# Products inside the attention steps, an out projection by halves of features, index scores inside chunks, rotations on GpSimd

## The reference, cut to what matters

```python
# layer 2 of the first model: chunked attention, 16 heads of 64
kv = rmsnorm(h, kv_norm_g) @ w_kv                  # [256, 2048]
q = (rmsnorm(h, b_norm_g) @ w_q) * 64 ** -0.5      # [256, 1024]
o = softmax(q @ k.T + bias) @ v;  h = h + o @ w_o
h = h + conv_ffn(rmsnorm(h, f_norm_g))
# second model, even layer: 8 "forgetting" heads and 8 sliding-window heads with sinks
fq, fk, fv, fgl, sq, sk, sv = split(h @ w_in)      # w_in [1024, 2312]
x = x + g_m * (concat(fox(fq, fk, fv, log_sigmoid(fgl)), swa(rope(sq), rope(sk), sv, sinks)) @ w_out)
# second model, odd layer: an index picks 64 keys for each query
q, k, v, iq, ik, iw = split(h @ w_in)              # w_in [1024, 2120]; q, k, iq, ik get rope
score = sum_over_8_index_heads(iw * relu(iq @ ik.T)); keys = top_k(score, 64)
x = x + g_m * (attention_over(keys) @ w_out)
x = x + g_f * mixture_of_experts(x)
# the gates g_*, shifts and scales of the second model: silu(c) @ ada_w + ada_b, 12288 columns
```

## Time and profile before

| | us |
|---|---|
| runs | 1716.73, 1739.09, 1742.68 |
| median | 1739.09 |
| the profiled execution | 1743.0 |
| its span | 1741.0 |
| mean granted TensorE clock in it | 0.909 of full |

### The profile page before, as it was taken

The page is one execution under the profiler, slowest core; times in us unless marked ns, Lnnn a source line. Parts: engine busy times, 40 slices in busy tenths (PEclk is TensorE's granted clock), DMA queues, the critical chain, the costliest instruction groups (busy, mean ns, idle before and its releaser), DMA issues.

```text
span 1741.0 us, 20071 instructions
## 1 busy us (share of the span) xinstructions
PE 1597.5 (92%) x7386; PEld 1316.0 (76%) x7387; DVE 1242.2 (71%) x1681; ACT 899.8 (52%) x1123; POOL 4.3 (0%) x16
## 2 busy tenths in 40 slices
PE   5899999988999999789899998969879999999995
PEld 4778877776878878678788887858767887788874
DVE  4757888655457887664678875684478888888887
ACT  4545553434346653444443334432357777777774
POOL 0000000000000000000000000000000000000000
PEclk9999999996699999895899999865789999999998
DMA  7544447663044448460267675310248888897882
GB/s 309 218 168 146 182 181 292 239 241 122 24 175 164 166 171 315 151 229 34 97 250 279 256 263 192 145 49 1 73 147 325 319 307 318 299 342 302 308 316 116
DMA packets 54264, 358.17 MB, mean 206 GB/s; under 512 B 7088, under 2 KB 8112, under 8 KB 13360
## 3 DMA queue, kind: packets, MB, share of 16 engines
q1 hardware_dynamic: 51392, 353.47, 54.6%
q0 software_dynamic: 144, 2.10, 0.3%
q10 hardware_dynamic: 2656, 1.64, 0.3%
HBM read 356.13 MB, written 1.05 MB: 205 GB/s over the span
## 4 chain that ended last, share of the span: by engine, by line
PE 74%; DVE 15%; ACT 5%; issue 5%; DMA 1%; PEldq 0%; DVEq 0%; PEld 0%; ACTq 0%; SPq 0%
PE ps L413 19%; PE ps L415 19%; PE ps L414 19%; DVE wlo L1293 5%; PE ps L572 4%; PE ps L592 3%; PE ps L581 2%; PE ps L775 2%; ACT whi L918 2%; PE ps L524 1%; DVE tok L1421 1%; DMA head_scratch<-w_s_dram 1%; DVE tok L1832 1%; PE ps L548 1%; ACT ps L930 1%
## 5 line engine op out<-in xcount | busy, mean ns | idle before, releaser
L1293 DVE TENSOR_TENSOR wlo<-raw,whi 128x2048 fp32r<-128x2048 f32 (+1 forms) x303 | 651.1, 2171 | 186.4 <-ACT whi L918 174.5
L918 ACT ACTIVATE whi<-raw 128x2048 fp32r<-128x2048 f32 (+1 forms) x303 | 546.8, 1822 | 294.2 <-PE ps L415 293.9
L413 PE MATMUL ps<-whi,xhi 128*128 128x512 f32 (+3 forms) x1360 | 537.5, 395 | 22.9 <-DVE xlo L1366 8.0
L415 PE MATMUL ps<-whi,xlo 128*128 128x512 f32 (+3 forms) x1360 | 526.4, 387 | 0.0
L414 PE MATMUL ps<-wlo,xhi 128*128 128x512 f32 (+3 forms) x1360 | 526.0, 387 | 0.0
L413 PEld LDWEIGHTS ps<-whi,xhi 128*128 128x128 f32 x1360 | 260.2, 191 | 80.0 <-DVE wlo L1293 12.0
L415 PEld LDWEIGHTS ps<-whi,xlo 128*128 128x128 f32 x1360 | 259.6, 191 | 52.4
L414 PEld LDWEIGHTS ps<-wlo,xhi 128*128 128x128 f32 x1360 | 260.7, 192 | 48.2
L413 PE MATMUL ps<-whi,ahi 128*128 128x512 f32 x440 | 178.3, 405 | 12.8 <-DVE wlo L1293 12.8
L414 PE MATMUL ps<-wlo,ahi 128*128 128x512 f32 x440 | 174.9, 398 | 0.0
L415 PE MATMUL ps<-whi,alo 128*128 128x512 f32 x440 | 174.8, 397 | 0.0
(11 more groups left out here) (230 smaller groups left out, 1265.9 us busy)
## 6 DMA issues: line engine op xcount, KB each, us to landing
raw<-stream_dram SPq DMA_DIRECT2D x318, 1024.0 KB, 5.2
raw<-stream_dram SPq DMA_DIRECT2D x30, 512.0 KB, 4.1
attn_scratch<-toep_dram POOLq DMA_DIRECT2D x1, 2048.0 KB, 7.9
raw<-stream_dram SPq DMA_DIRECT2D x2, 528.0 KB, 5.7
h<-x_dram SPq DMA_DIRECT2D x1, 1024.0 KB, 5.5
y<-tok SPq DMA_DIRECT2D x2, 512.0 KB, 2.7
head_scratch<-w_s_dram ACTq DMA_DIRECT2D x1, 512.0 KB, 18.5
gates<-fg_dram ACTq DMA_DIRECT2D x1, 512.0 KB, 21.7
```

What stands on the lines that cost most here:

```text
L413: pe.matmul(o, xh, wh, start=start, stop=False)
L415: return pe.matmul(o, xl, wh, start=False, stop=stop)
L918: act.activation(whi[:, q % SPL, 0:w], raw[:, s % RAW, 0:w], ACT.Copy).then_inc(sem("hi_done"), 1)
L1293: dve.tensor_tensor(wlo[:, q % SPL, 0:w], raw[:, s % RAW, 0:w], whi[:, q % SPL, 0:w].bitcast(F32), ALU.subtract).then_inc(sem("lo_done"), 1)
```

## The change

1. **Products inside the steps (C and E).** PE's `product` is cut into `begin` and `half` (one slot for one token tile, 12 matmuls). The projections are reordered so that what the first heads need comes first: q, then k and v by halves in C; window heads before forgetting heads in E. The chunks that only later heads need run inside the steps: 10 halves in steps 0 to 8 of C, 8 halves in steps 0 to 6 of E. Their results are copied out by ACT and transposed by PE inside the steps too. Since the pairs of banks 0 to 3 are now taken by products, scores and value products have one bank each (4 and 5), and `back` uses bank 6, which `turn` uses for every second head. ACT and DVE split the slots inside the steps, at the place `split(base + slots_before(halves, i) + SPL)`.
2. **Out projection by halves of features.** Its weights are stored so that the first two slots hold the 512 features of the first two groups of heads for both output chunks. Two of its eight halves run in steps 16 and 18, and `residual_out` adds the results.
3. **Index scores inside chunks (O).** The order is index keys (the chunk of 72 columns), index queries, k and v, q, q. The 16 index products come in four groups of four inside and behind the slots of the chunks of k and v and of the first q.
4. **Rotations on GpSimd.** The rotations of q and k in O (12 instructions of 128x128 and 24 of 128x256) and of one token tile in E (6 of 128x320) are done by POOL, and POOL also makes `wlo` of the two slots of the last chunk in O.
5. **The "a" slots** move: none is left in the out projections, fewer in kv and `e_in`, more in the two first down projections (8 each where there were 6) and in the down projection of E (10 of its 12 slots where there were 6).

In the diff, a line that is only "..." marks what is left out.

```diff
-O_ORDER = (3, 4, 0, 1, 2)
+O_ORDER = (4, 3, 2, 0, 1)
+KV_ORDER = (0, 2, 1, 3)
...
-        proj("gmlp_in", 2 * D, G_ORDER, layer=0, first=4)
-        proj("gmlp_out", D, layer=0)
+        proj("gmlp_in", 2 * D, G_ORDER, layer=0, with_ada=(3, 5, 7))
+        proj("gmlp_out", D, layer=0, with_ada=(1, 3))
         proj("up0", 2 * FF)
-        proj("down0", D, kt=FK, layer=0)
-        proj("kv", 2 * D, layer=0)
-        proj("q", D, layer=0)
-        proj("attn_out", D, layer=0)
+        proj("down0", D, kt=FK, layer=0, with_ada=(0, 1, 3, 4, 6, 7, 9, 10))
+        proj("q", D, layer=0, with_ada=(1, 3))
+        proj("kv", 2 * D, KV_ORDER, layer=0, with_ada=(1,))
+        proj("attn_out", D)
         proj("up1", 2 * FF)
-        proj("down1", D, kt=FK, layer=0)
+        proj("down1", D, kt=FK, layer=0, with_ada=(0, 1, 3, 4, 6, 7, 9, 10))
         assert not left[0]
-        proj("e_in", E_IN, E_ORDER, layer=1)
-        proj("e_out", D, layer=1)
-        proj("e_up", 2 * FF, layer=1)
-        proj("e_down", D, kt=FK, layer=1)
+        proj("e_in", E_IN, E_ORDER, layer=1, with_ada=(1, 3, 5))
+        proj("e_out", D)
+        proj("e_up", 2 * FF, layer=1, with_ada=range(1, 22, 2))
+        proj("e_down", D, kt=FK, layer=1, with_ada=(0, 1, 2, 3, 4, 6, 7, 8, 9, 10))
...
+        HALVES_C = {0: 2, 1: 1, 2: 1, 3: 1, 4: 1, 5: 1, 6: 1, 7: 1, 8: 1, 16: 1, 18: 1}
+        HALVES_E = {0: 2, 1: 1, 2: 1, 3: 1, 4: 1, 5: 1, 6: 1, 16: 1, 18: 1}
+        HALVES_O = {16: 1, 18: 1}
+        o_slots = [QAT["o_in"] + sum(len(slots_of(KT, w)) for _, w in chunks_of(O_IN, O_ORDER)[:n]) for n in range(6)]
+        POOL_LO = range(o_slots[4], o_slots[5])
+        def slots_before(halves, i):
+            return sum(k for step, k in halves.items() if step < i) // 2
...
+            def lo_of(q):
+                s = PL.s_of[q]
+                g.wait_ge(sem("lo_done"), s)
+                g.wait_ge(sem("hi_done"), q + 1)
+                g.tensor_tensor(wlo[:, q % SPL, :], raw[:, s % RAW, :], whi[:, q % SPL, :].bitcast(F32), ALU.subtract)\
+                    .then_inc(sem("lo_done"), 1)
+            g.wait_ge(sem("acc_free"), PL.cat["o_in"] + 3)
+            rotate(1024, 4)
+            g.sem_inc(sem("rot_k"), 1)
+            for q in POOL_LO:
+                lo_of(q)
+            for n in range(2):
+                g.wait_ge(sem("acc_free"), PL.cat["o_in"] + 4 + n)
+                rotate(n * W, 8)
+                g.sem_inc(sem("rot_q"), 1)
...
                 def scores(u):
-                    if u >= 2:
-                        pe.wait_ge(sem("att_m"), b + u - 1)
+                    if u:
+                        pe.wait_ge(sem("att_m"), b + u)
                     a = units[u]
                     for t in range(NT):
-                        m = pe.matmul(ps[:, 2 * sc + u % 2, parts(t)], a["q"][:, t * P:(t + 1) * P], a["k"][:, 0:(t + 1) * P],
-                                      start=True, stop=True)
+                        m = pe.matmul(ps[:, 4, parts(t)], a["q"][:, t * P:(t + 1) * P], a["k"][:, 0:(t + 1) * P], start=True, stop=True)
...
                 def values(u):
                     pe.wait_ge(sem("att_c"), b + u + 1)
-                    g = u // 4
-                    if u % 4 == 0 and g >= 2:
-                        pe.wait_ge(sem("att_on"), bg + g - 1)
+                    if u and u % 4 == 0:
+                        pe.wait_ge(sem("att_on"), bg + u // 4)
                     for t in range(NT):
...
+                out = []
                 for i in range(n + 3):
                     if i < n:
+                        if i == 8 and turned:
+                            pe.wait_ge(sem("tr_free"), T("tr"))
                         scores(i)
+                    work(i)
+                    if i == 16:
+                        pe.wait_ge(sem("att_o"), bg + 2)
+                        out = [begin(W, first=first), begin(W, first=first)]
+                        half(out[0], 0)
+                    if i == 18:
+                        half(out[0], 1)
                     if 0 <= i - 2 < n:
                         turn(i - 2)
                     if 0 <= i - 3 < n:
                         values(i - 3)
+                    if i in (7, 11, 15):
+                        back(i // 4 - 1)
+                    ends(i)
                 T.up("att", n)
+                half(out[1], 0)
+                back(3)
+                half(out[1], 1)
+                pe.wait_ge(sem("att_o"), bg + 4)
+                for t in range(NT):
+                    half(out[0], t)
+                for t in range(NT):
+                    half(out[1], t, early=t == 0)
...
+            def other_heads(i):
+                if i == 0:
+                    half(chunk_now[0], 0)
+                    half(chunk_now[0], 1)
+                if i in (1, 5):
+                    chunk_now[0] = begin(W)
+                if 1 <= i <= 8:
+                    half(chunk_now[0], (i - 1) % 2)
+            def other_keys(i):
+                if i in (2, 5):
+                    pe.wait_ge(sem("acc_free"), T("acc", 1))
+                if i == 10:
+                    pe.wait_ge(sem("acc_free"), T("acc"))
+                if i in (5, 6):
+                    two(TB, i - 3, i - 3)
+            attention(CHUNKED, OUT_C, pT_c, other_heads, other_keys, (5, 6))
...
+                    before(i)
+                    if i in (8, 12, 16):
                         hi(i // 4 - 2)
-                hi(2)
-                split(used[0] + SPL)
+                    if i < n:
+                        exps(i)
+                    split(base + slots_before(halves, i) + SPL)
+                    after(i)
...
                 for i in range(n + 3):
                     if i < n:
                         mask(i)
+                    if i in (8, 12, 16):
+                        lo(i // 4 - 2)
                     if 0 <= i - 2 < n:
                         copy(i - 2)
-                    if i >= 7 and i % 4 == 3:
-                        weigh(i // 4 - 1)
-                    if i >= 9 and i % 4 == 1:
-                        lo(i // 4 - 2)
-                weigh(3)
-                split(used[0] + SPL)
+                    if i in (6, 10, 14, 18):
+                        weigh((i - 6) // 4)
+                    split(base + slots_before(halves, i) + SPL)
...
-            rotate(W, 8)
-            dve.sem_inc(sem("rope_done"), 1)
             thr = lambda t: mx8[:, t, 7:8]
             both(lambda t, nk: dve.tensor_tensor(score[:, t, 0:nk], score[:, t, 0:nk], causal[:, S - nk:S], ALU.add))
             for n in range(TOPK // 8):
@@ -1719,10 +1918,6 @@
                 both(lambda t, nk: dve.max(mx8[:, t, :], src[:, t, 0:nk]))
                 if n < TOPK // 8 - 1:
                     both(lambda t, nk: dve.match_replace(left[:, t, 0:nk], mx8[:, t, :], src[:, t, 0:nk], GONE))
-                if n == 3:
-                    rotate(2 * W, 4)
-                    dve.sem_inc(sem("rope_done"), 1)
-            skip(1)
```

514 lines of the change are left out of this document (311 added, 203 removed).

## The result

| | before | changed |
|---|---|---|
| runs, us | 1716.73, 1739.09, 1742.68, 1742.17 | 1774.32, 1768.42, 1773.08, 1768.20 |
| median, us | 1740.63 | 1770.75 |
| profiled execution, its span, us | 1743.0, 1741.0 | 1774.32, 1772.6 |
| mean granted clock | 0.909 | 0.917 |

The changed kernel is slower: the ratio is 1.022, 95% interval 1.012 to 1.033, and nothing of the interval reaches 1 (whether it is slower by more than 2% the interval leaves open). The forecast was 1733, at most 1758. The kernel before falls in two groups of times, 1713 to 1717 us (12 of its 55 runs in all comparisons here, middle 1715) and 1738 to 1744 (the other 43); its trace and all its medians are from the upper one, and the ratio mixes the two. All four times of the changed kernel lie above all 55: 30 us above the median of the kernel before, and 56 above 1715.

The account below looks back on a forecast made before the run. PE was taken as the bound, through many small float32 matmuls at half clock. C +9, E -2, O +1.4 and "a" slots -2 sum to +6.4: 1736.6, or 1733 against the median; range 1718 to 1748, chance 0.53.

Parts of the forecast that it names:

- PE bound by small matmuls at half clock: Steps of C and O, also E: PE's rows busy nearly all the time at 0.50, a C step 3.58 us.
- halves that hold the clock: Steps 0 to 8 of C: product halves keep full clock, 18.6 us net where 27 before, +8.5.
- The waits where the cover ends: Step 9 in C and 7 in E: late mask behind a split no longer hidden by products, about 2.9 each.
- POOL's price: POOL's work taken at about twice DVE's time: 4.6 us for `wlo`, 0.8 a rotation.
- The wait for a third split in O: O: scores of head 2 wait for mask 1 behind a third split, coming about 1156.5, leaving +8.
- What the halves of the out projections cost: Steps 16 and 18: halves fill no idle time; the first meets half clock, -1.0 each in C and E.
- C, before the steps: C ahead of its attention steps: a shorter wait in the projections, +1.2, and less turning of blocks, +4.0.
- Other down projections have room: 0: Down projections other than E's: more "a" slots there cost nothing, 0.
- -2 for E's: Down projection of E: four more "a" slots at 3.1 make DVE busy 58.7 of 60 us, costing 2.
- O, +1.4: Stage O: earlier first mask leaves +8, less q rounds -2.2, two waits -3.9 and tail -0.5.
- POOL is late: Rival for O, chance 0.12: at four times DVE's prices POOL delays the first mask by 17 us, 1750.
- the clock stays up without products: Rival, chance 0.17: later steps of C and E stay at full clock after the products end, 1716.

Follow-up runs that it names:

- e2_csplit: Changed kernel with ACT making the next weight slot's high part ahead of each of two turned-block copies in C's q chunks; 1760.42 us.
- e5_turn: Changed kernel with PE's sum over an "a" slot pair made behind the first half of a weight slot, not the second; 1762.62 us.
- e1_plan: Changed kernel with four "a" slots moved from the down projection of E to its up projection; 1772.18 us.
- e3_dvelo: Changed kernel with both POOL `wlo` splits of O's last chunk given to DVE, inside its search; 1767.12 us.
- b1_plan: Kernel before with only the changed kernel's "a" slot places from E on; 1722.37 us.
- b2_plan: Kernel before with one "a" slot (behind slot 7) moved from E's input projection to its down projection; 1711.76 us.
- e10_ahead: Changed kernel with the eight halves of E made ahead of its attention steps, not inside them; 1786.92 us.
- b4_c: b2_plan plus other "a" slot places in C and q's last blocks all turned behind an earlier slot; 1708.29 us.
- e9_hold: Changed kernel with `xhi` and `xlo` a step earlier, DVE's splits a step later, and splits of steps 7 to 12 held to step 13; 1755.52 us.
- e11_all: Changed kernel with the edits of e2_csplit, e5_turn and e9_hold, and POOL's splits in O cut in four; 1739.21 us.
- b5_best: b4_c with e5_turn's early sum, the changed kernel's first-stage "a" places, and "a" slots at 0, 1, 2 of q; 1739.76 us.
- E experiment: Any follow-up run that alters the changed kernel (median 1770.75 us), rather than the kernel before.

## Why the prediction was wrong

**Right.** PE bound by small matmuls at half clock, and halves that hold the clock: without the ten halves steps 0 to 8 of C took 19.2 (394.73 to 441.43 less 27.5) for the 18.6 forecast, at 0.96. The waits where the cover ends: 2.9 said, 3.49 in C; in E they came as one of 5.42, for which 2.9 and 1.7 were said. POOL's price: 4.7 for a split (4.6 said), 0.74 for a rotation (0.8 said). The wait for a third split in O: 4.05 under the 5 given. What the halves of the out projections cost was not read apart.

**"C, before the steps", +5.2.** This step failed: it cost 9.9 instead, 15 of the miss. I costed the "a" slots there, which DVE alone carries, and never wrote down what ACT and PE do in a row: turn, wait for PE's slot, split. e2_csplit shows it: 15 us in the trace, with 5.0 of the 5.2 back. The rest of C came a little better than forecast.

**"Other down projections have room: 0", and -2 for E's.** This step failed as well: they cost 9.0 and 13.0, 20 of the miss. DVE's busy time was right (58.7 said; in 1010 to 1082 it is the 59.29 of the row below), the conclusion from it was not: an engine in strict order with 98% of its time booked cannot also wait, and I had left out its waits for PE's sum, 14.9 us.

```profile
1010.00:1082.00 72.00, 66.05 (x299) 53.30 (x298) 59.29 (x68) 19.96 (x13) 0.00 (x0) 0.95 0.73 272
```

The two first down projections got two "a" slots more each, at 3.1; they lost 5.6 and 3.4 of those 6.2. No run took the slots away there, so for these two the cause is inferred; e5_turn left them nearly as they were (-1.4 and +0.1). e1_plan shows that the up projection of E had no room for four more either. The rows that would have told were in the earlier trace rows: a `wlo` that waits mostly for `whi` is time that "a" work can't simply fill, since the `whi` waits for PE.

**O, +1.4.** It lost 6.9. The search was to start 11.9 earlier than before; with all that stands before moved by 21.2 it started 1.9 earlier (1158.67 - 21.2 = 1137.5, and 1139.4). Of the missing 10, 8.6 is DVE behind POOL (10.70 against 2.15 in e3_dvelo). The mask behind the search lost 2.5 more beside POOL's rotations (7.9 against 5.4). The scores of head 2 came 4.0 us later in the stage (1189.73 less 1103.06, against 1164.52 less 1081.89) where 8 earlier was forecast; the rest of the stage took back 3.7 of these 12. Runs without an edit in O put its loss between 4.5 and 6.9. My rival "POOL is late" had the shared port, but priced it as a delay of POOL, "two such DVE splits inside POOL's work". It fell on the other side: DVE's short instructions wait for POOL's long ones. Ahead of E's wait of 4.13 the same is seen.

**The clock.** The halves do hold it, but "the clock stays up without products" (0.17) can be true in E, even without the change: b1_plan and b2_plan have the same small matmuls at 1.00 for 30 us. So the 10 to 16 us that halves save in E (e10_ahead) are less than the 28 that the old order gives when its clock stays up. The prediction set what the Trainium skill, "TensorE: Matmul & The Clock Gate", Part 4, says of the PE-mode transpose beside the busy rows at 0.50. As an explanation of the half clock it is not borne out: the steps of b2_plan have the same three transposes each, and they keep full clock.

**Left open.** What decides between the two levels: it is not PE's idle time in the steps (b4_c's C 55.00 of 55 at half, b2_plan's E 28.95 of 30 at full), and not a wait just ahead alone. In C, e9_hold and e11_all both fall for 3 to 4 us behind a wait of 1.76, come back, and then both wait 0.84 (at 446.48 and 433.75): the first stays up, the second falls. In E, b1_plan and b5_best have the same two waits ahead of the scores (0.72 and 0.77 or 0.78): the first stays up, the second falls 3 us behind them. The 3.5 of the experts and the rest is mostly that one trace: every E experiment is 2.3 to 3.2 shorter there.

## What to carry to other kernels

Before work is moved onto an engine that runs in strict order, write down the row of waits and work around the new place, on all engines of the circle; busy share says only what it can't do. A long POOL instruction can cost DVE its whole length, so cut it short, or place it beside DVE work that the trace shows unslowed (here `max` and `match_replace`, but not `tensor_scalar`, which has one tensor too), and look at what DVE does behind it before counting the gain. And before filling a half-clock stretch with products, look whether what stands ahead of it has lost the clock: here one "a" slot moved made every run about as fast as the kernel before is in 12 of 55 (1712 us, 29 below its median), and the whole rearrangement with five faults mended ended at 1739.

## What the runs showed of the hardware

- Chains of small float32 matmuls stay at either clock level, with the same instructions: 53 us at 0.50 in b5_best, 30 us at 1.00 in b2_plan. One program can do both: the kernel before has runs of 1715 and of 1741, and E's steps at the other level would be worth just that (an inference, since no trace is from the lower group).
- DVE and POOL shut each other out for whole instructions, both ways (10.70 for 2.15, 2.51 for 0.5). Not every DVE instruction is touched. A `tensor_scalar` of 128x512 took 1.03 us for 0.48 beside POOL's rotation, and the mask of O 7.9 for 5.4. The search was not slowed; its maxima, DVE from 1158 to 1180 in the changed kernel (352 ns before):

```profile
L1918 DVE MAX8 mx<-attn_scratch 128x8 f32<-128x128 f32 (+1 forms) x16 | 5.0, 351 | 0.3
```

- Cutting POOL's 2048 columns in four costs POOL 13% (9.38 to 10.64) and takes DVE's four additions from 10.70 to 4.06 us (the two behind them rose from 1.58 to 2.67).
